# Early front of layer 1 in a two-layer hybrid encoder step: per-head pieces moved from half steps to whole steps, three heads under way, PSUM copies on ScalarE

## The reference, cut to what matters

```python
def layer(x, pos0, ...):
    h = rmsnorm(x, norm1_g)
    xa, ga, xq, qf, kf, vf, gates = jnp.split(h @ w_in, cuts, axis=-1)
    xc, conv_state = causal_conv(xa, conv_hist, conv_w, conv_b)
    ha, lru_state = rg_lru(xc, lru_h0, lru_wa, lru_ba, lru_wx, lru_bx, lru_L)
    ya = ha * jax.nn.gelu(ga, approximate=False)
    yb, pool_state = pool_mixer(xq, pool_hist, pos0, pool_w, pool_scale)
    q, k = rotary(qf ...), rotary(kf ...)            # 8 heads, 2 x 64 wide each
    o = diff_attn(q, k, v, chunk mask or past keys)  # softmax 1 - lam * softmax 2, times v
    yc = rmsnorm(o, subln_g) * (1.0 - lam_init)
    m = g[0] * (ya @ proj_a) + g[1] * (yb @ proj_b) + g[2] * (yc @ proj_c)
    x = x + m @ w_out
    return x + peer(rmsnorm(x, norm2_g), ...)

def expert_block(xb, ib, gb):                        # 8 heads x 16 picks a frame
    act = gelu(einsum('nd,nhkd->nhk', xb, u[ib]))
    return einsum('nhk,nhkd->nd', gb * act, v[ib])
```

## Time and profile before

| | before |
|---|---|
| median of three runs | 2632.62 us |
| the profiled execution's own time | 2632.88 us |
| its span, first to last instruction | 2631.0 us |
| mean granted TensorE clock | 0.87 |
| busy share of the span: PE, DVE, ACT, POOL | 74%, 60%, 27%, 30% |
| HBM traffic over the span | 331 GB/s |
| steps 59 to 79 of layer 0, by their Gelus | 376.3 us |

### The profile page before, as it was taken

One profiled execution on the slowest core, in us unless ns is written; L12 is line 12 of the kernel. 1 busy time (PEld: TensorE's weight loads), 2 busy tenths in 40 slices (PEclk: granted clock), 3 DMA queues, 4 the chain that ended last, 5 costly groups with the idle time before them and its releaser, 6 DMA issues.

```text
span 2631.0 us, 31937 instructions
## 1 busy us (share of the span) xinstructions
PE 1945.1 (74%) x10932; PEld 1107.3 (42%) x10932; DVE 1591.6 (60%) x4381; ACT 716.3 (27%) x1784; POOL 787.9 (30%) x895
## 2 busy tenths in 40 slices
PE   7999988886777548665665778988886777555555
PEld 6556876653433115222222547866652332111111
DVE  3553165667789777745444341265667889787764
ACT  3422133322233232422222321233313232222121
POOL 0121023333333333323233020033334334444442
PEclk9999999998888779887877899999998888777787
DMA  6135769999999999876666547499999999999996
GB/s 198 63 133 184 271 279 418 417 413 420 413 384 404 414 370 398 330 287 252 234 260 253 194 166 274 178 418 417 409 419 420 412 377 406 421 400 421 421 421 284
DMA packets 163776, 871.72 MB, mean 331 GB/s; under 512 B 20288, under 2 KB 42816, under 8 KB 79648
## 3 DMA queue, kind: packets, MB, share of 16 engines
q0 software_dynamic: 95424, 676.62, 63.0%
q1 hardware_dynamic: 68192, 193.08, 20.1%
HBM read 862.92 MB, written 6.71 MB: 331 GB/s over the span
## 4 chain that ended last, share of the span: by engine, by line
DMA 24%; PE 20%; DVE 20%; issue 13%; PEld 6%; PEldq 4%; DVEq 4%; POOL 4%; ACT 3%; ACTq 0%; POOLq 0%; SPq 0%
DMA MIX_RINGS<-in_peer_uv_dram,IDX 17%; DVE MIX_RINGS L2143 5%; PEldq L1160 4%; PEld ps L984 4%; DMA WQKV_E<-in_peer_uv_dram,IDX 3%; PE ps L934 3%; DVEq L1987 3%; PE ps L916 3%; POOL MIX_RINGS L862 3%; PE ps L1158 3%; DMA W<-in_peer_uv_dram,IDX 3%; DVE W L2143 2%; PE ps L1408 2%; PEld ps L1047 1%; PE ps L944 1%
## 5 line engine op out<-in xcount | busy, mean ns | idle before, releaser
L1158 PE MATMUL ps<-MIX_RINGS,GC 64*64 64x512 f32 x3344 | 688.3, 746 | 322.4 <-ACT GC L1618 310.5
L862 POOL DMA_INDIRECT MIX_RINGS<-in_peer_uv_dram,IDX x418 | 446.4, 1068 | 903.6 <-PEq L1160 577.7
L1158 PE MATMUL ps<-W,GC 64*64 64x512 f32 x1296 | 369.1, 783 | 223.4 <-ACT GC L1618 218.8
L1158 PEld LDWEIGHTS ps<-MIX_RINGS,GC 64*64 64x64 f32 x3344 | 165.8, 161 | 658.7 <-ACT GC L1618 335.2
L2143 DVE CUSTOM_DVE_ANT_0 MIX_RINGS<-MIX_RINGS 128x1024 f32<-128x1024 f32 x242 | 289.2, 1222 | 63.5 <-DMA MIX_RINGS<-in_peer_uv_dram,IDX 57.0
L1618 ACT ACTIVATE GC<-twins,WV 128x64 f32<-128x64 f32 x640 | 170.2, 336 | 533.3 <-DVEq L2156 533.0
L2143 DVE CUSTOM_DVE_ANT_0 MIX_RINGS<-MIX_RINGS,WQKV_E 128x1024 f32<-128x1024 f32 x176 | 212.5, 1225 | 151.7 <-DMA MIX_RINGS<-in_peer_uv_dram,IDX 145.5
L862 POOL DMA_INDIRECT W<-in_peer_uv_dram,IDX x162 | 171.8, 1060 | 365.4 <-PEq L1160 311.3
L1158 PEld LDWEIGHTS ps<-W,GC 64*64 64x64 f32 x1296 | 86.4, 169 | 399.7 <-ACT GC L1618 215.6
L1610 ACT ACTIVATE GV<-AV 128x4 f32<-128x4 f32 x160 | 32.8, 205 | 630.2 <-DVEq L2144 629.7
L984 PE MATMUL ps<-HT,W 128*128 128x192 f32 x768 | 146.6, 353 | 41.7 <-issue 25.6
(11 more groups left out here) (477 smaller groups left out, 3021.0 us busy)
## 6 DMA issues: line engine op xcount, KB each, us to landing
W<-in_merge_w_dram SPq DMA_DIRECT2D x40, 1024.0 KB, 4.9
W<-in_merge_w_dram SPq DMA_DIRECT2D x60, 512.0 KB, 14.6
WQKV_E<-in_qkv_w_dram SPq DMA_DIRECT2D x16, 1536.0 KB, 7.0
W<-in_query_w_dram SPq DMA_DIRECT2D x16, 1024.0 KB, 11.5
W<-in_w_in_dram SPq DMA_DIRECT2D x12, 1024.0 KB, 9.8
W<-in_query_w_dram SPq DMA_DIRECT2D x20, 512.0 KB
W<-in_out_w_dram SPq DMA_DIRECT2D x8, 1024.0 KB, 17.0
MIX_RINGS<-in_peer_uv_dram,IDX POOLq DMA_INDIRECT x418, 12.8
```

Source lines behind the costliest of these rows:

```text
L862: pool.indirect_dma_start(UV[r], None, table, bass.IndirectOffsetOnAxis(IDX[:, n % DEEP, j:j + 1], 0))\
L1158: pe.matmul(ps[o:o + CHUNK, n:n + 512], w[r, :], v[r, d * 512:(d + 1) * 512], start=False, stop=False, skip_group_check=True)
```

## The change

Pieces are now numbered by whole steps, u = s - 50, and `early(u)` is called once in each step: on PE ahead of `experts`, on ACT behind the diagonals, on DVE behind `dots`. Head k starts at u = 9 + 2k. In its even steps (u - 9 even) PE does the values of head k-3, the scores of head k-1 and both halves of the product of head k; in its odd steps the transposed weights of head k-2 and the transposes of Q and K of head k. The engine that takes a result up does so later in the step or a step later. DVE's copies out of PSUM (K transposed, transposed weights, outputs) go to ACT, merged with ACT's own (384 and 320 columns); V is copied into buffers of its own, three deep; banks are shared out anew. The norm is split: heads 0 to 6 in the last two steps, head 7 and the transposes of all outputs behind step 79. The input blocks of the recurrence come before those of its gate; the first units of layer 1's late front use other slots and wait for step 77 and for the last head's values.

```diff
-A_SLOT = 100
-A_HEADS = 19
-A_PACE = 4
...
+A_STEP = 50
+A_HEADS = 9
...
-A_ROTARY = [4 * ((A_SLOT + A_HEADS + A_PACE * _h + 1) // 2) + 8 for _h in range(HEADS)]
+A_ROTARY = [GROUP * (A_STEP + A_HEADS + 2 * _h) + 12 for _h in range(HEADS)]
...
-                    sp.wait_ge(*sso_ready.at(EARLY, 1))
-                    for u in range(3):
+                    for par in range(2):
+                        sp.wait_ge(*kv_out[par].at(EARLY, 4 * HEADS // 2))
+                    sp.wait_ge(*uv_free.at(0, PICKS - 8))
+                    for u in range(2):
                         ff_unit(u)
+                    sp.wait_ge(*att_done.at(EARLY, HEADS))
+                    ff_unit(2)
...
+                k, odd = divmod(u - A_HEADS, 2)
+                if k >= 0 and odd == 0:
+                    if k >= 3:
+                        early_values(k - 3)
+                    if 1 <= k <= HEADS:
+                        early_scores(k - 1)
+                    if k < HEADS:
+                        early_qkv(k)
+                if k >= 0 and odd:
+                    if 2 <= k < HEADS + 2:
+                        early_weights(k - 2)
+                    if k < HEADS:
+                        early_turn(k)
...
-                    if l == 0 and 2 * s >= A_SLOT:
-                        early(2 * s - A_SLOT)
+                    if l == 0 and s >= A_STEP:
+                        early(s - A_STEP)
                     experts(l, s)
-                    if l == 0 and 2 * s >= A_SLOT:
-                        early(2 * s + 1 - A_SLOT)
...
+            def early_copies(h, o):
...
+                for i, (t, r, qk, v) in enumerate(((0, P, A_ZH, A_VH), (2, DEC_SEQ, A_ZS, A_VS))):
+                    if h < HEADS:
+                        act.wait_ge(*z_ps.at(EARLY, 3 * h + 2 + i))
+                        act.activation(qk[:, h % 2, :], bank(i, 0, 2 * HW)[0:r], ACT.Copy)
+                    if o >= 0:
+                        act.wait_ge(*att_done.at(EARLY, o + 1))
+                        act.activation(A_OALL[t][0:r, o, :], bank(i, 3 * HW, 4 * HW)[0:r], ACT.Copy)
+                    if h < HEADS:
+                        act.activation(v[:, h % 3, :], bank(i, 2 * HW, 3 * HW)[0:r], ACT.Copy)
+                        act.drain().then_inc(z_ev.sem, 1)
+                if o >= 0:
+                    act.drain().then_inc(o_ev.sem, 1)
...
+                k, odd = divmod(u - A_HEADS, 2)
+                if odd == 0 and 2 <= k < HEADS + 2:
+                    early_weights(k - 2)
+                if odd and 1 <= k < HEADS + 1:
+                    early_highest(k - 1)
+                if odd and 3 <= k < HEADS + 3:
+                    early_sums(k - 3)
...
                 dve.drain().then_inc(layer_done.sem, 1)
+                if l + 1 < DEPTH:
+                    early_sums(HEADS - 1)
+                    dve.drain().then_inc(sso_ready.sem, 1)
                 add_experts(l, 1)
+                if l + 1 < DEPTH:
+                    early_norm(1)
```

More of the change, by code:

```diff
@@ L811, in early_rotary @@
                 par = h % 2
-                kcol, vcol = slice(HW, 2 * HW), slice(2 * HW, 3 * HW)
+                kcol = slice(HW, 2 * HW)
                 pool.wait_ge(*z_ev.at(EARLY, 2 * h + 1))
@@ new lines, in early_scores @@
+            def early_scores(h):
+                d = [slice(m * HD, (m + 1) * HD) for m in range(2)]
+                pe.wait_ge(*qt_ev.at(EARLY, h + 1))
+                pe.wait_ge(*(ex_done.at(EARLY, 4 * h) if h else sig_ev.at(EARLY, 2 * RC)))
+                for m in range(2):
+                    pe.matmul(bank(2 + m, 0, P), A_QT[d[m], 0:P], A_KT[d[m], 0:P], start=True, stop=True,
+                              skip_group_check=True).then_inc(s_ps.sem, 1)
+                pe.wait_ge(*cache_in[0].at(EARLY, h + 1))
+                for m in range(2):
+                    pe.matmul(bank(2 + m, P, P + PAST)[0:DEC_SEQ], A_QT[d[m], P:P + CHUNK], CK[1][d[m], :],
+                              start=True, stop=True, skip_group_check=True)
+                for m in range(2):
+                    pe.matmul(bank(2 + m, P + PAST, P + PAST + DEC_SEQ)[0:DEC_SEQ], A_QT[d[m], P:P + CHUNK],
+                              A_KT[d[m], P:P + CHUNK], start=True, stop=True, skip_group_check=True)\
+                        .then_inc(s_ps.sem, 1)
@@ new lines, in early_root, with early_outputs @@
+            def early_root(i):
+                hs = (slice(0, HEADS - 1), slice(HEADS - 1, HEADS))[i]
+                act.wait_ge(*sso_ready.at(EARLY, i + 1))
+                for t in (0, 2):
+                    act.activation(rso[:, t, hs], sso[:, t, hs], ACT.Sqrt, bias=eps_c[:, :], scale=1.0 / HW)
+                act.drain().then_inc(sso_root.sem, 1)
+            def early_outputs():
+                for par in range(2):
+                    act.wait_ge(*kv_out[par].at(EARLY, 4 * HEADS // 2))
+                for hh in range(HEADS):
+                    act.wait_ge(*yt_ps.at(EARLY, hh + 1))
+                    act.activation(YT[:, 2 * RC + hh, A_COLS], bank(hh % 4)[:, A_COLS], ACT.Copy, scale=SUBG[:, 0:1])\
+                        .then_inc(yt_ev.sem, 1)
@@ new lines, in early_sums, with early_norm @@
+            def early_sums(h):
+                dve.wait_ge(*o_ev.at(EARLY, h + 1))
+                for i, t in enumerate((0, 2)):
+                    dve.tensor_tensor(A_SQ[:, i], A_OALL[t][:, h, :], A_OALL[t][:, h, :], ALU.mult)
+                fence()
+                dve.tensor_reduce(sso[:, 0:3:2, h], A_SQ, AX_X, ALU.add)
+            def early_norm(i):
+                hs = (slice(0, HEADS - 1), slice(HEADS - 1, HEADS))[i]
+                dve.wait_ge(*sso_root.at(EARLY, i + 1))
+                for t in (0, 2):
+                    dve.reciprocal(sso[:, t, hs], rso[:, t, hs])
+                fence()
+                for t in (0, 2):
+                    dve.tensor_tensor(A_OALL[t][:, hs, :], A_OALL[t][:, hs, :],
+                                      sso[:, t, hs].unsqueeze(2).to_broadcast([P, hs.stop - hs.start, HW]), ALU.mult)
+                dve.drain().then_inc(on_ready.sem, 1)
@@ L2720 @@
     proj_ab = _np.concatenate([inputs["proj_a"], inputs["proj_b"]], axis=1)
-    order = [2 * RC + i for i in range(RC)] + [RC + i for i in range(RC)] + list(range(RC))
+    order = [2 * RC + i for i in range(RC)] + list(range(RC)) + [RC + i for i in range(RC)]
     rows["early_w"] = blocks(inputs["w_in"][1:2, :, 0:COL_Q])[:, order]
```

487 lines of the change are left out of this document (220 added, 267 removed).

## The result

The changed kernel takes 2530.5 us (median of 4 runs) where the kernel before takes 2634.1 in runs beside it: a ratio of 0.9608, 95% interval 0.9591 to 0.9625, 103.7 us less. Its profiled execution took 2529.96 us (span 2528.1), 102.9 less than that of before. Forecast were 2515 us and 117.5 less.

The account below looks back on a forecast made before the run. A chain of waits inside single steps was taken to bound steps 59 on. Eight heads at 27.0 us plus 41.6 for steps 75 to 78 replace 376.3 by 257.6; with +1.2 at the layer's end, 2515 us, range 2493 to 2566.

Parts of the forecast that it names:

- rival (e): Heads: links between engines within a step (product-copies, rotation-transposes, transposes-copies) keep the period near 42, time near 2632; chance 0.03.
- A head's period: Steps 59 to 74: PE's work 23.9 plus 2.4 standing, DMA 25.9, some loss: 27.0 us a head, 216.0 for eight.
- rotates for 2.7 ... PE stands for 2.4 us: In each head POOL's rotation of Q and K ends at T+7.2 (T: product's end on PE); PE waits 2.4 us.
- at the clock of such a burst: PE's 23.9 us of work a head runs at 0.92 granted clock, as in one dense burst.
- DMA as the second limit: Each head moves 10.42 MB, at 403 GB/s 25.9 us, close to PE's 26.3.
- The late unit loads: Layer 1's first units load behind step 77 and during step 79, beside the last gathers: 0, at worst 5 us.
- DMA covers them at 0.99: Steps 50 to 58: already memory bound, later pieces lie under DMA: 0, some 5 us either way if not.
- The layer's end: Behind step 79: head 7's scaling stands on the norm's chain, ACT's output copies fit its idle time: +1.2 us.
- (b): Heads: rotation held up by two gathers or slow issue, PE stands 5 us, 29.0 to 29.5 a head, 2533; chance 0.13.
- (a): Heads and steps 75 to 78: DMA does not reach 403 GB/s with this mix, 28.3 a head, 2530; chance 0.14.
- (c): Heads: PE's clock stays at 0.78, each head leaving PE a 2.4 us gap, 2563 us; chance 0.12.
- (d): Heads: PE falls to 1.2 GHz throughout, 50.2 us a head, slower than before at 2701 us; chance 0.04.

Follow-up runs that it names:

- the fastest run: Changed kernel with the rotation two gathers earlier, its stores two later, and DVE weighing gates ahead of routing from the first head's step: 2500.2 us, ratio 0.9498.
- the run with those pieces alone: Kernel before with only the new pieces of steps 50 to 62 (input blocks, pool, recurrence), heads as they were: 2626.6 us, ratio 0.9969.
- weighing first: DVE weighs gates before its routing pieces: 2529.7 us in the changed kernel, 2500.2 in the one with rotation earlier and stores later (2510.9 without).

## Why the prediction was right and where it failed

**What bound the kernel, and that spreading frees it: right.** In steps 61 to 74 the chain waits of PE and DVE are gone as said (DVE's for scores and weights are under 10 us), and the run that puts one copy back into a same-step chain loses a third of the gain. Of rival (e)'s three links left, it is rotation to transposes that still binds.

**A head's period: mis-sized, 29.4 instead of 27.0 us, and with steps 75 to 78 22.0 us over the sum.** PE's own work was right: 23.9 forecast, 23.5 measured in heads without a stand. Two numbers beside it were not. The step "rotates for 2.7 ... PE stands for 2.4 us" took its duration from a rotation of the kernel before that had no dot product beside it; in the new place DVE's dot products run, the rotation takes 4.1 and PE stands 4.1. And the step "at the clock of such a burst" let the new order be one dense burst, while the stand splits it: the experts behind it take 5.3 to 6.5 us instead of 4.0. With both, 23.9 + 4.1 + 1.8 = 29.8, near the measured 29.4 by steps and 29.9 between products. Where the rotation kept its own duration (the run with held dot products), a head took 27.3 us by steps, still a microsecond over the 26.3 worked out for a stand of that length, and the experts behind it were slow: the second failure doesn't hang on the first.

**DMA as the second limit: right, and not yet reached.** 25.9 us a head at 403 GB/s were counted; the fastest run reaches 24.9 at 401 GB/s and share 1.00. Its fourteen steps moved 69.9 MB, 10.0 a head instead of the 10.42 counted, which would take 26.0 at that rate. In steps 75 to 78 the forecast 41.6 became 44.5 us: 18.1 MB moved there, where only 16.8 MB of gathers were counted; three loads of layer 1's units, 1 MB each, are issued there. The late unit loads, costed at 0 with 5 at worst, are in this term.

**Steps 50 to 58: 0 forecast, -9.1 in the profiles, some -8 by the run with those pieces alone.** The step that failed is "DMA covers them at 0.99": the mean of the stretch hid two holes. Cut into 40 slices of 2.9 us, that stretch of the kernel before shows them, one of 268 and 123 GB/s and one of 254; after the change no slice is under 391:

```profile
GB/s 429 424 426 429 415 424 424 268 123 385 415 428 425 412 431 405 414 436 414 418 417 424 418 418 410 418 426 408 426 411 410 419 419 427 420 421 424 424 254 393
```

The holes are worth some 4 us (what these slices lack at 418 GB/s). The remainder of the 9.1 shows as bytes: 47.4 MB moved in these steps before, 45.3 after. Why the front moves fewer bytes across the stretch's ends was not tried.

**The layer's end: +1.2 forecast, +5.6 measured behind step 79, most of it not there.** From the Gelu of step 79 to the next layer's first late input product it is 20.6 us, 19.1 before: +1.5, the term as priced. The chain runs through head 7's scaling, as said:

```profile
1368.98 0.28 DVE L2571 TENSOR_TENSOR MIX_RINGS<-MIX_RINGS,sso 128x128 f32<-128x128 f32 x1
...
1369.47 1.22 DVE L2732 CUSTOM_DVE_ANT_0 MIX_RINGS<-X 128x1024 f32<-128x1024 f32 x1 [0.21 <-issue]
...
1375.38 0.98 PE L1383 MATMUL ps<-HT,W 128*128 128x128 f32 x3 [0.73 <-issue]
```

The other 4 us are scattered over layer 1 and stay open. The stretch up to step 50, in which nothing is changed, came out at 967 to 976 us in the profiles of these runs, so differences of a few us between single profiles say little.

**The total: closer than its terms.** The miss of 14.6 us is +22.0 in steps 59 to 78 and +4.4 behind step 79, against -9.1 in steps 50 to 58 and -2.7 ahead of step 50, which were put at nothing. That these two came out the other way is luck. Of the signs put on record, DVE's waits under 10 us and about 1 us more at the layer's end came. The head's period, DMA's share and rate, PE's 2 to 3 us for the rotation and the 117 us of steps 50 to 58 didn't, and the granted clock is at its mark of 0.90. The head's period stands just under the 30 us that were to prove the prediction wrong.

**The rivals.** (b) had the place and nearly the numbers, a stand of 5 us, 29.0 to 29.5 a head, 2533, but another cause: the gathers ahead of the rotation leave at T+2.2 and T+3.4 as forecast, and DVE holds the rotation. (a) gives 2530 too, and is out, since the fastest run moves 401 GB/s at 1.00 in the same steps. The Trainium skill's 358 GB/s a core (DMA: Bandwidth & Descriptors, "Where 436 GB/s comes from"), taken as the bound of this one core, is out by the same row. (c) is out as stated (0.90, not 0.78), but its remark that each head leaves PE a gap was the second half of the miss. (d) didn't come, and (e) only in the run with the copy given back, and there in part.

## What to carry to other kernels

A duration read from a trace holds for what ran beside it: before moving an instruction of GpSimd, look at what VectorE does in the new place. Where PE has one wait left in an otherwise dense period, price the work behind the wait at the lower clock too: in these runs stands of 2 to 5 us were followed by experts at 5.2 to 6.9 us instead of 4.0 in all heads but one. And when one wait is removed, read the trace again before adding the next edit: weighing first moved nothing while the rotation bound, and some 6 to 11 us, not firmly measured, once it did not.

## What the runs showed that was not expected

The prediction had none of these. Useless work can pay: 16 products more a head, 3.7 us of them, made the kernel some 10 us faster, because they kept the granted clock at 1.00. Holding VectorE back paid as well, 12 us. A mean DMA share of 0.99 over 118 us left room for some 8 us.
